# Full expert tiles: one 512-column product for u's high part against both token parts, score halves added on VectorE, high parts made on ScalarE

## The chip, the cores and the metric

One NeuronCore of a Trainium2 chip runs the whole program. The metric is the device time of one execution in microseconds, the median of several runs. The profile beside it is one execution taken by the hardware profiler.

## The reference

256 tokens of 1024 channels pass one block of attention and feed-forward, and then two layers that each end in a PEER stage. The change lies in the PEER stage. There each token has 8 heads that choose 16 of 16384 experts each; an expert is a row of `u_emb` and a row of `v_emb`, 1024 long:

```python
s = jnp.einsum('thpk,hpnk->thpn', q, sub_keys).astype(jnp.float32)
sv, si = lax.top_k(s, K)
...
gate = jax.nn.softmax(fv, axis=-1)
u = u_emb[eidx]
v = v_emb[eidx]
act = jax.nn.gelu(jnp.einsum('thkd,td->thk', u, x_t).astype(jnp.float32), approximate=False)
return jnp.einsum('thk,thkd->td', (gate * act).astype(x_t.dtype), v)
```

All arrays are float32.

## The kernel before, in words

The kernel gathers nothing. It holds a dense table of gates, 256 tokens by 16384 experts, that is zero where an expert wasn't chosen, and computes every expert for every token. The experts are cut into 128 tiles (TILES) of 128. For a tile j the work is: scores, the product of the tile's u (128 experts x 1024) and the tokens HT (1024 x 256), in 8 steps of 128 channels; Gelu; the product with the tile's gates; values, the product of these activations and the tile's v (128 x 1024), added up in four PSUM banks over all 128 tiles.

For float32 accuracy at the speed of the rounded type (fp32r), an operand is kept as a high part, which is the operand rounded by a copy, and a low part, which is the operand less the high part. A product of two such operands is three matmuls, high by high, high by low and low by high. `in_parts` (L505 is its matmul) issues them. The scores of a full tile are thus 8 x 3 matmuls with 256 columns (the tokens), written to the first half of PSUM bank 4 + j % 2. The values are 4 x 3 matmuls with 512 columns.

A layer's first 26 tiles (EARLY) are treated in another way: their scores are plain float32 products, computed while the experts are being chosen and while the gates are built, and only their values are in parts. The 102 tiles behind them (LATE) are the full tiles: scores and values both in parts. They run in loops of six tiles per turn (STEP) on each engine.

The order of the work in the full tiles is written by hand for each engine:

- TensorE: scores of j+1, values of j, scores of j+2, values of j+1, and so on. Scores wait for the semaphore `expert_u`, values for `expert_gated` and `expert_v`.
- ScalarE (L1216): the Gelu of tile j from PSUM once `expert_scored` tells of it. Nothing else.
- VectorE (`expert`): for tile j, the product with the gates (L1892); the high part of u of tile j+2 once its load has arrived (a cast, `high`, L1799); the high part of the activations; the low part of u of j+2 (`low`, L1803); the low part of the activations, which counts `expert_gated`; then, once values of j-1 are done, the high part and the low part of v of tile j+1.
- SyncE (`load_experts`) issues the loads, 512 KB each: u of n (L2171) once scores of n-3 are done, then v of n (L2178) once values of n-3 are done, then u of n+1, and so on in this one queue.

u and v have three buffers each (E_SLOTS); the low part is written over the loaded operand. The high parts have two buffers each. Plain and rounded names (`ring` and `ring_rounded`, `HN` and `HN_rounded`, `HT` and `HT_rounded`) are the same memory under two types. In `ring`, columns 0 to 3D are u, 3D to 6D v, 6D to 8D the high parts of u, 8D to 10D those of v, 10D to 12D the high part of HT (D is 1024). HN holds the activations and, behind them, `g2_row`. HN and HT are neighbours in memory.

In the early tiles ScalarE makes the high parts of v (L1206), VectorE the low parts.

## Time and profile before

| what | value |
|---|---|
| median of 3 runs | 2453.8 us |
| runs | 2455.82, 2448.6, 2453.8 us |
| profiled execution, span | 2448.3 us |
| TensorE matmul busy | 2366.7 us, 97% |
| VectorE busy | 1939.3 us, 79% |
| ScalarE busy | 547.8 us, 22% |
| mean granted TensorE clock | 0.992 |
| full tiles of layer 1 | from 813 to 1389 us of the span |
| full tiles of layer 2 | from 1858 to 2434 us of the span |

The span runs from the first to the last instruction of the profiled execution; of that execution the profile gives the span alone, and the runs' times lie 0.3 to 7.5 us above it. Busy times are sums over the span. Rows of a timeline give the start in us from the span's start, the duration in us, the engine, the source line, the operation, what it writes and reads, and in brackets how long the engine was idle ahead of it and which work released it. Matmuls are pipelined, so a row with several of them gives the time from the first's start to the last's end, and the spacing of the starts is what one costs in a stream.

### The profile page before, as it was taken

The numbers are of one execution on the slowest core, as the hardware profiler recorded it, in microseconds if no ns is written. First come the engines' busy times: TensorE is split into PE (matmuls) and PEld (weight loads), VectorE is DVE, ScalarE is ACT, GpSimd is POOL, SyncE is SP. The second block draws the span as 40 slices with busy tenths as digits, with TensorE's granted clock in tenths as the row PEclk, the third lists the DMA queues.
The fourth block names the chain that finished last, engine by engine and source line by source line (L and its number), as shares of the span: only waits on it lengthen the run. The fifth ranks groups of instructions, "written<-read, shape, count | busy, mean of one in ns | idle before, by whom it ended". The sixth has DMA issues, their size and how long they took to land.

```text
span 2448.3 us, 38882 instructions
## 1 busy us (share of the span) xinstructions
PE 2366.7 (97%) x14368; PEld 2061.1 (84%) x14368; DVE 1939.3 (79%) x3972; ACT 547.8 (22%) x962; POOL 298.2 (12%) x228
## 2 busy tenths in 40 slices
PE   8998999999999999999999998999999999999998
PEld 7766998669887899999999877698978999999997
DVE  5445887769997888888888766399987888888887
ACT  4433332222333100000000236223331000000001
POOL 0000000026580000000000000266800000000000
PEclk9999999999999999999999999999999999999999
DMA  7324888853215455555555550232154555555553
GB/s 270 150 78 155 301 325 332 338 226 130 87 36 198 164 187 183 186 184 187 188 188 188 207 186 35 103 121 88 43 180 164 188 187 184 184 185 187 187 188 129
DMA packets 97731, 430.08 MB, mean 176 GB/s; under 512 B 11232, under 2 KB 11872, under 8 KB 90720
## 3 DMA queue, kind: packets, MB, share of 16 engines
q1 hardware_dynamic: 97632, 428.75, 48.6%
q8 instruction: 63, 1.03, 0.2%
q14 instruction: 36, 0.29, 0.0%
HBM read 427.66 MB, written 1.05 MB: 175 GB/s over the span
## 4 chain that ended last, share of the span: by engine, by line
PE 83%; DVE 13%; ACT 2%; DMA 1%; issue 1%; SPq 0%; DVEq 0%; ACTq 0%; PEldq 0%
PE ps L505 66%; PE ps L550 5%; PE ps L773 4%; DVE HN L1785 4%; DVE HN L1783 3%; PE ps L563 3%; PE ps L600 1%; PE ps L621 1%; DVE arena L1795 1%; PE ps L735 1%; DVE ring_rounded L1803 1%; PE ps L799 1%; ACT arena L1012 1%; DMA ring<-in_stream 1%; DVE ring_rounded L1374 1%
## 5 line engine op out<-in xcount | busy, mean ns | idle before, releaser
L505 PE MATMUL ps<-ring_rounded,HN_rounded 128*128 128x512 f32 (+1 forms) x3104 | 751.2, 391 | 8.6 <-DVE ring_rounded L1803 5.2
L505 PEld LDWEIGHTS ps<-ring_rounded,HN_rounded 128*128 128x128 f32 x3104 | 567.0, 188 | 127.2 <-issue 15.0
L505 PE MATMUL ps<-ring_rounded 128*128 128x256 f32 x3264 | 619.4, 283 | 0.0
L1803 DVE TENSOR_TENSOR ring_rounded<-ring,ring_rounded 128x1024 fp32r<-128x1024 f32 x460 | 561.9, 1222 | 19.2 <-ACT ring_rounded L1206 12.0
L505 PEld LDWEIGHTS ps<-ring_rounded 128*128 128x128 f32 x3264 | 522.3, 191 | 7.9
L505 PE MATMUL ps<-HT_rounded,ring_rounded 128*128 128x256 f32 x1632 | 461.8, 283 | 0.0
L1799 DVE CAST ring_rounded<-ring 128x1024 fp32r<-128x1024 f32 x406 | 280.5, 691 | 151.3 <-DMA ring<-in_experts_u 149.4
L505 PEld LDWEIGHTS ps<-HT_rounded,ring_rounded 128*128 128x128 f32 x1632 | 312.5, 191 | 7.9
L1216 ACT ACTIVATE HN<-ps 128x256 f32<-128x256 f32 x204 | 78.5, 385 | 1061.7 <-PE ps L505 1061.7
L505 PE MATMUL ps<-parts 128*128 128x256 f32 (+2 forms) x1184 | 249.2, 301 | 1.9 <-DVE parts L1369 1.5
L773 PE MATMUL ps<-HT,ring 128*128 128x256 f32 x832 | 202.5, 381 | 1.4 <-ACT arena L982 1.4
L505 PEld LDWEIGHTS ps<-parts 128*128 128x128 f32 x1184 | 192.1, 189 | 12.8 <-DVE parts L1369 2.0
L2120 POOL TENSOR_TENSOR ring_rounded<-ring,parts 128x1024 fp32r<-128x1024 f32 x8 | 18.8, 2376 | 1375.8 <-ACT parts L1158 1375.8
L2134 POOL TENSOR_SCALAR HN<-iota,slots_t 128x128 f32<-128x128 f32 x128 | 177.5, 1389 | 64.2 <-DVEq L1775 36.2
L773 PEld LDWEIGHTS ps<-HT,ring 128*128 128x128 f32 x832 | 148.9, 192 | 16.6 <-ACT arena L982 1.8
L505 PE MATMUL ps<-parts,ring_rounded 128*128 128x256 f32 x576 | 162.3, 282 | 0.0
L1374 DVE TENSOR_TENSOR ring_rounded<-ring,parts 128x4096 fp32r<-128x4096 f32 (+2 forms) x28 | 117.5, 4198 | 44.5 <-ACT parts L1005 44.0
L799 PEld LDWEIGHTS ps<-HN 128*128 128x128 f32 x1024 | 131.5, 194 | 24.0 <-issue 13.7
L799 PE MATMUL ps<-HN 128*128 128x128 f32 x1024 | 141.1, 282 | 7.2 <-DVE HN L1785 5.8
L1892 DVE TENSOR_TENSOR HN<-HN,arena 128x256 f32<-128x256 f32 x204 | 130.6, 640 | 16.1 <-ACT HN L1216 11.1
L550 PE MATMUL ps<-ring,HT 128*128 128x512 f32 (+1 forms) x320 | 136.2, 586 | 0.0
L982 ACT ACTIVATE arena<-ps 128x512 f32<-128x512 f32 (+4 forms) x136 | 77.3, 580 | 221.5 <-PE ps L505 144.9
(254 smaller groups left out, 2566.8 us busy)
## 6 DMA issues: line engine op xcount, KB each, us to landing
ring<-in_experts_u SPq DMA_DIRECT2D x256, 512.0 KB, 4.2
ring<-in_experts_v SPq DMA_DIRECT2D x256, 512.0 KB, 3.5
ring<-in_stream SPq DMA_DIRECT2D x45, 2048.0 KB, 8.8
arena<-in_ada SPq DMA_DIRECT2D x96, 512.0 KB, 7.2
arena<-in_keys SPq DMA_DIRECT2D x2, 1024.0 KB, 13.9
ring<-in_stream SPq DMA_DIRECT2D x1, 1792.0 KB, 7.9
ring<-in_stream SPq DMA_DIRECT2D x1, 1664.0 KB, 8.1
ring<-in_stream SPq DMA_DIRECT2D x1, 1040.0 KB, 19.1
```

Source lines behind the costliest of these rows:

```text
L505: mm = pe.matmul(out_, p, q, start=(first and i == 0), stop=(last and i == 2))
L550: mm = pe.matmul(t[:, 0:n], src[:, k, b * P:(b + 1) * P], w[:, k, :], start=(k == 0), stop=(k == nk - 1))
L773: mm = pe.matmul(ps[:, 4 + n % 2, 0:T], pre_u[:, n % P_SLOTS, k * P:(k + 1) * P], HT[:, k, :], start=(k == 0), stop=(k == KT - 1))
L799: mm = pe.matmul(ps[:, 6 + u, t * P:(t + 1) * P], hot[:, u, 1, t, :], hot[:, u, 0, t, :], start=True, stop=True)
L982: ins = act.activation(dst, t if src is None else src(t), func)
L1216: act.activation(act_e[:, a, :], ps[:, 4 + a, 0:T], ACT.Gelu).then_inc(sem("expert_act"), 1)
L1374: dve.tensor_tensor(weights_low(name), weights(name)[:, 0:IN_PARTS_SIZE[name]], weights_high(name).bitcast(F32), ALU.subtract).then_inc(se ...
L1785: ins = dve.tensor_scalar(hot[:, u, 1, t, :], iota, slots_t[:, 1, at_ + t:at_ + t + 1], slots_t[:, 2, at_ + t:at_ + t + 1], ALU.is_equal, ...
L1799: return dve.tensor_copy(dst, src)
L1803: return dve.tensor_tensor(dst, src, h.bitcast(F32), ALU.subtract)
L1892: dve.tensor_tensor(act_e[:, j % 2], act_e[:, j % 2], g, ALU.mult).then_inc(sem("split_steps"), 1)
L2134: pool.tensor_scalar(hot[:, g % 2, 1, GROUP - 1, :], iota, slots_t[:, 1, t:t + 1], slots_t[:, 2, t:t + 1], ALU.is_equal, ALU.mult).then_in ...
```

## The change

In the full tiles:

- `HN_rounded` and `HT_rounded` become one tensor, so that one operand (`ht_both`) can name both token parts: the high part moves from `ring` to HN, the low part stays in HT. For each of the 8 channel steps the high part of u meets both token parts in one matmul of 512 columns, which fills a whole PSUM bank: the first half has high by high, the second half high by low. The low part of u meets the high token part in a matmul of 256 columns that is added to the first half. So 24 matmuls of 256 columns become 8 of 512 and 8 of 256.
- The two halves still have to be added. ScalarE copies the second half to SBUF (`half_s`), VectorE adds the first half to it, and the Gelu works on that sum in SBUF.
- The high parts of u (tile j+2) and of v (tile j+1) are made by ScalarE instead of VectorE.
- ScalarE's order for tile j is now: half copy, wait for u of j+2 and its high part, Gelu, wait for v of j+1 and its high part. VectorE's order is: low part of v of j, the add, the low part of u of j+2, the product with the gates, the high part and the low part of the activations.
- The activations and the half copy now lie in `ring` from 10D on, and `g2_row` in `arena`.

SyncE's program isn't changed.

```diff
--- before.py
+++ after.py
@@ -142,7 +142,8 @@
                   ("arena", T * NKEYS))
         with ExitStack() as whole_floats:
             hn_flat, ht_flat, ring, arena = [whole_floats.enter_context(nc.sbuf_tensor(name, [P, n], F32))[:, :] for name, n in shared]
-        hn_r, ht_r, ring_r = [sb(f"{name}_rounded", n, F32R)[:, :] for name, n in shared[:3]]
+        hnht_r, ring_r = sb("HNHT_rounded", NB * D + KT * T, F32R)[:, :], sb("ring_rounded", SLOTS * SLOT, F32R)[:, :]
+        hn_r, ht_r = hnht_r[:, 0:NB * D], hnht_r[:, NB * D:]
         parts_at = 13600
         act_parts_r = sb("act_parts", 2 * FT * T, F32R)[:, :]
         sb("arena_before", parts_at - 2 * FT * T)
@@ -465,14 +466,15 @@
         exp_vh = r3(ring_r[:, 8 * D:10 * D], 2)
         meanwhile = r3(ring[:, 0:3 * D], GATE_TILES)
         pre_u = r3(ring[:, 6 * D:10 * D], P_SLOTS)
-        ht_high = r3(ring_r[:, 10 * D:12 * D], KT)
-        ht_low = r3(ht_r, KT)
-        act_e = r3(hn_flat[:, 0:512], 2)
-        act_l = r3(hn_r[:, 0:512], 2)
-        act_h = r3(hn_r[:, 512:1024], 2)
-        g2_row = hn_flat[:, 1024:2048]
+        ht_high, ht_low = r3(hn_r, KT), r3(ht_r, KT)
+        ht_both = hnht_r.rearrange("p (a k t) -> p a k t", a=2, k=KT)
+        act_e = r3(ring[:, 10 * D:10 * D + 512], 2)
+        act_l = r3(ring_r[:, 10 * D:10 * D + 512], 2)
+        act_h = r3(ring_r[:, 10 * D + 512:11 * D], 2)
+        half_s = r3(ring[:, 11 * D:11 * D + 512], 2)
         g2_diag = arena[:, 0:D]
         end_diag = arena[:, D:2 * D]
+        g2_row = arena[:, 2 * D:3 * D]
         hot = hn_flat.rearrange("p (u a t n) -> p u a t n", u=2, a=2, t=GROUP)
         NG = T // GROUP
 
@@ -811,10 +813,11 @@
                 def expert_scores(j, ready):
 
                     pe.wait_ge(sem("expert_u"), ready)
+                    t = ps[:, 4 + j % 2, :]
                     for k in range(KT):
                         c = slice(k * P, (k + 1) * P)
-                        mm = in_parts(ps[:, 4 + j % 2, 0:T], (exp_uh[:, j % 2, c], exp_ul[:, j % E_SLOTS, c]),
-                                           (ht_high[:, k, :], ht_low[:, k, :]), k == 0, k == KT - 1)
+                        pe.matmul(r3(t, 2), exp_uh[:, j % 2, c], ht_both[:, :, k, :], start=(k == 0), stop=False)
+                        mm = pe.matmul(t[:, 0:T], exp_ul[:, j % E_SLOTS, c], ht_high[:, k, :], start=False, stop=(k == KT - 1))
                     mm.then_inc(sem("expert_scored"), 1)
 
                 def expert_values(j, ready, first=False, last=False, low=None):
@@ -1198,22 +1201,48 @@
                             keep_scores(n)
                     if g == NG - 6:
                         act.wait_ge(sem("expert_v0_arrived"), 16 * (l * len(range(0, TILES, E_SLOTS)) + 1))
-                        act.activation(exp_vh[:, 0], exp_v[:, 0], ACT.Copy).then_inc(sem("early_v_high"), 1)
+                        act.activation(exp_vh[:, 0], exp_v[:, 0], ACT.Copy).then_inc(sem("v_high"), 1)
                 for n in range(1, EARLY + 1):
                     act.wait_ge(sem(f"expert_v{n % E_SLOTS}_arrived"), 16 * (l * len(range(n % E_SLOTS, TILES, E_SLOTS)) + n // E_SLOTS + 1))
                     if n >= 2:
                         act.wait_ge(sem("expert_used"), l * (TILES + 1) + n)
-                    act.activation(exp_vh[:, n % 2], exp_v[:, n % E_SLOTS], ACT.Copy).then_inc(sem("early_v_high"), 1)
+                    act.activation(exp_vh[:, n % 2], exp_v[:, n % E_SLOTS], ACT.Copy).then_inc(sem("v_high"), 1)
                     if SPLIT_AT <= n < SPLIT_AT + KT:
                         k = n - SPLIT_AT
                         act.activation(ht_high[:, k], HT[:, k], ACT.Copy).then_inc(sem("ht_high"), 1)
                     if n == G2_AT + 2:
                         act.wait_ge(sem("g2_spread"), l + 1)
                         act.activation(g2_row, ps[:, 6:8, :].rearrange("p a n -> p (a n)"), ACT.Copy).then_inc(sem("g2_row"), 1)
-                with act.Fori(0, LATE // 2) as i:
-                    for a in range(2):
-                        act.wait_ge(sem("expert_scored"), i * 2 + (l * TILES + EARLY + a + 1))
-                        act.activation(act_e[:, a, :], ps[:, 4 + a, 0:T], ACT.Gelu).then_inc(sem("expert_act"), 1)
+
+                def expert(j, turn=None):
+
+                    def at_(n, each=1):
+                        return n if turn is None else turn * (STEP * each) + n
+
+                    def arrived(kind, n):
+
+                        count = 16 * (l * len(range(n % E_SLOTS, TILES, E_SLOTS)) + n // E_SLOTS + 1) if kind == "v" else \
+                            16 * (l * LATE // E_SLOTS + (n - EARLY) // E_SLOTS + 1)
+                        act.wait_ge(sem(f"expert_{kind}{n % E_SLOTS}_arrived"), count if turn is None else turn * (16 * STEP // E_SLOTS) + count)
+
+                    act.wait_ge(sem("expert_scored"), at_(l * TILES + j + 1))
+                    act.activation(half_s[:, j % 2], ps[:, 4 + j % 2, T:2 * T], ACT.Copy).then_inc(sem("half_stored"), 1)
+                    if j + 2 < TILES:
+                        arrived("u", j + 2)
+                        act.activation(exp_uh[:, j % 2], exp_u[:, (j + 2) % E_SLOTS], ACT.Copy).then_inc(sem("u_high"), 1)
+                    act.wait_ge(sem("expert_summed"), at_(l * LATE + j - EARLY + 1))
+                    act.activation(act_e[:, j % 2], act_e[:, j % 2], ACT.Gelu).then_inc(sem("expert_act"), 1)
+                    if j + 1 < TILES:
+                        arrived("v", j + 1)
+                        act.wait_ge(sem("expert_used"), at_(l * (TILES + 1) + j + 1))
+                        act.activation(exp_vh[:, (j + 1) % 2], exp_v[:, (j + 1) % E_SLOTS], ACT.Copy).then_inc(sem("v_high"), 1)
+
+                turns = (LATE - 2) // STEP
+                with act.Fori(0, turns) as i:
+                    for j in range(STEP):
+                        expert(EARLY + j, i)
+                for j in range(EARLY + turns * STEP, TILES):
+                    expert(j)
                 load_table(ACT.Sqrt)
 
 
@@ -1818,7 +1847,7 @@
                 def early_v_low(n):
 
                     v_arrived(n)
-                    dve.wait_ge(sem("early_v_high"), l * (EARLY + 1) + n + 1)
+                    dve.wait_ge(sem("v_high"), l * TILES + n + 1)
                     low(exp_vl[:, n % E_SLOTS] if low_in_place(n) else exp_uh[:, n % 2], exp_v[:, n % E_SLOTS], exp_vh[:, n % 2]).then_inc(sem("expert_v"), 1)
 
                 def split_ht_part(k):
@@ -1877,48 +1906,38 @@
                         diagonal(f"g2_{l}", g2_diag, mod(l, 5))
                         if l == 1:
                             diagonal("end2", end_diag, col("final_norm_2"), factor=-0.5)
-                dve.wait_ge(sem("expert_used"), base_v + EARLY)
-                early_v_low(EARLY)
-
-                def expert(j, turn=None, more_u=True, more_v=True):
+
+                def expert(j, turn=None):
 
                     def at_(n, each=1):
                         return n if turn is None else turn * (STEP * each) + n
 
                     n = at_(j - CHOICE_TILES)
-                    done = split_base + 4 * (j - EARLY)
+                    done = 2 * (l * LATE + j - EARLY)
+                    e = act_e[:, j % 2]
+                    v, vl, vh = exp_v[:, j % E_SLOTS], exp_vl[:, j % E_SLOTS], exp_vh[:, j % 2]
+                    dve.wait_ge(sem("v_high"), at_(base + j + 1))
+                    low(vl, v, vh).then_inc(sem("expert_v"), 1)
+                    dve.wait_ge(sem("half_stored"), at_(l * LATE + j - EARLY + 1))
+                    dve.tensor_tensor(e, ps[:, 4 + j % 2, 0:T], half_s[:, j % 2], ALU.add).then_inc(sem("expert_summed"), 1)
+                    if j + 2 < TILES:
+                        u, ul, uh = exp_u[:, (j + 2) % E_SLOTS], exp_ul[:, (j + 2) % E_SLOTS], exp_uh[:, j % 2]
+                        dve.wait_ge(sem("u_high"), at_(l * (LATE - 2) + j - EARLY + 1))
+                        low(ul, u, uh).then_inc(sem("expert_u"), 1)
                     dve.wait_ge(sem("expert_act"), at_(l * LATE + j - EARLY + 1))
                     g = gates[:, :, bass.ds(n, 1)].rearrange("p t o -> p (t o)") if turn is not None else gates[:, :, n]
-                    dve.tensor_tensor(act_e[:, j % 2], act_e[:, j % 2], g, ALU.mult).then_inc(sem("split_steps"), 1)
-                    if more_u:
-                        u, ul, uh = exp_u[:, (j + 2) % E_SLOTS], exp_ul[:, (j + 2) % E_SLOTS], exp_uh[:, j % 2]
-                        u_arrived(j + 2, turn)
-                        high(uh, u).then_inc(sem("split_steps"), 1)
-                    dve.wait_ge(sem("split_steps"), at_(done + 1, 4))
-                    high(act_h[:, j % 2], act_e[:, j % 2]).then_inc(sem("split_steps"), 1)
-                    if more_u:
-                        dve.wait_ge(sem("split_steps"), at_(done + 2, 4))
-                        low(ul, u, uh).then_inc(sem("expert_u"), 1)
-                    dve.wait_ge(sem("split_steps"), at_(done + 2 + more_u, 4))
-                    low(act_l[:, j % 2], act_e[:, j % 2], act_h[:, j % 2]).then_inc(sem("expert_gated"), 1)
-                    if more_v:
-                        v, vl, vh = exp_v[:, (j + 1) % E_SLOTS], exp_vl[:, (j + 1) % E_SLOTS], exp_vh[:, (j + 1) % 2]
-                        v_arrived(j + 1, turn)
-                        dve.wait_ge(sem("expert_used"), at_(base_v + j + 1))
-                        high(vh, v).then_inc(sem("split_steps"), 1)
-                        dve.wait_ge(sem("split_steps"), at_(done + 3 + more_u, 4))
-                        low(vl, v, vh).then_inc(sem("expert_v"), 1)
-
-                split_base = l * (4 * LATE - 3)
+                    dve.tensor_tensor(e, e, g, ALU.mult).then_inc(sem("split_steps"), 1)
+                    dve.wait_ge(sem("split_steps"), at_(done + 1, 2))
+                    high(act_h[:, j % 2], e).then_inc(sem("split_steps"), 1)
+                    dve.wait_ge(sem("split_steps"), at_(done + 2, 2))
+                    low(act_l[:, j % 2], e, act_h[:, j % 2]).then_inc(sem("expert_gated"), 1)
+
                 turns = (LATE - 2) // STEP
                 with dve.Fori(0, turns) as i:
                     for j in range(STEP):
                         expert(EARLY + j, i)
-                for j in range(EARLY + turns * STEP, TILES - 2):
+                for j in range(EARLY + turns * STEP, TILES):
                     expert(j)
-                expert(TILES - 2, more_u=False)
-                split_base -= 1
-                expert(TILES - 1, more_u=False, more_v=False)
                 dve.wait_ge(sem("expert_used"), (l + 1) * (TILES + 1))
                 dve.wait_ge(sem("g2_row"), l + 1)
                 for b in range(NB):
```

## Rows read from the trace of the kernel before

**Rows 1.** The page, the chain that ended last, by line

```profile
PE ps L505 66%; PE ps L550 5%; PE ps L773 4%; DVE HN L1785 4%; DVE HN L1783 3%; PE ps L563 3%; PE ps L600 1%; PE ps L621 1%; DVE arena L1795 1%; PE ps L735 1%; DVE ring_rounded L1803 1%; PE ps L799 1%; ACT arena L1012 1%; DMA ring<-in_stream 1%; DVE ring_rounded L1374 1%
```

**Rows 2.** The chain in order of time: start, duration, what

```profile
813.13 575.97 PE ps L505 x3684
```

**Rows 3.** Stretches: length, busy us PE, PEld, DVE, ACT, POOL, clock, DMA share, GB/s

```profile
740.00:813.00 73.00, 70.78 (x308) 54.91 (x307) 60.33 (x98) 28.96 (x33) 0.00 (x0) 1.00 0.59 196
813.00:1389.00 576.00, 576.00 (x3687) 525.47 (x3686) 485.39 (x709) 41.77 (x105) 0.00 (x0) 1.00 0.51 182
...
1884.00:2434.00 550.00, 550.00 (x3514) 501.51 (x3514) 466.89 (x682) 38.81 (x99) 0.00 (x0) 1.00 0.52 183
```

**Rows 4.** Timeline of TensorE, one period of the full tiles

```profile
1001.30 2.91 PE L505 MATMUL ps<-ring_rounded,HN_rounded 128*128 128x512 f32 x12
1004.04 0.28 PE L505 MATMUL ps<-ring_rounded 128*128 128x256 f32 x1
...
1006.92 2.91 PE L505 MATMUL ps<-ring_rounded,HN_rounded 128*128 128x512 f32 x12
1009.66 0.28 PE L505 MATMUL ps<-ring_rounded 128*128 128x256 f32 x1
```

**Rows 5.** Groups by form, 815 to 1387: busy us, mean ns, idle before

```profile
L1803 DVE TENSOR_TENSOR ring_rounded<-ring,ring_rounded 128x1024 fp32r<-128x1024 f32 x201 | 245.7, 1222 | 3.5
...
L1216 ACT ACTIVATE HN<-ps 128x256 f32<-128x256 f32 x102 | 39.3, 385 | 530.6 <-PE ps L505 530.6
```

**Rows 6.** Timeline of the SP queue, full tiles

```profile
1005.11 0.33 SPq L2171 DMA_DIRECT2D ring<-in_experts_u  x1
1009.86 0.33 SPq L2178 DMA_DIRECT2D ring<-in_experts_v  x1
1010.39 0.33 SPq L2171 DMA_DIRECT2D ring<-in_experts_u  x1
```

**Rows 7.** Timeline of ScalarE and VectorE, full tiles

```profile
1007.12 0.38 ACT L1216 ACTIVATE HN<-ps 128x256 f32<-128x256 f32 x1 [5.24 <-PE ps L505]
...
1013.26 0.64 DVE L1892 TENSOR_TENSOR HN<-HN,arena 128x256 f32<-128x256 f32 x1
1014.55 0.69 DVE L1799 CAST ring_rounded<-ring 128x1024 fp32r<-128x1024 f32 x1 [0.65 <-DMA ring<-in_experts_u]
...
1016.50 0.42 DVE L1803 TENSOR_TENSOR HN_rounded<-HN,HN_rounded 128x256 fp32r<-128x256 f32 x1
```

**Rows 8.** Timeline of a tile of layer 2 with a late u

```profile
1881.34 0.69 DVE L1799 CAST ring_rounded<-ring 128x1024 fp32r<-128x1024 f32 x1 [2.24 <-DMA ring<-in_experts_u]
...
1883.28 0.42 DVE L1803 TENSOR_TENSOR HN_rounded<-HN,HN_rounded 128x256 fp32r<-128x256 f32 x1
...
1883.76 3.01 PE L505 MATMUL ps<-ring_rounded,HN_rounded 128*128 128x512 f32 x12 [0.24 <-DVE HN_rounded L1803]
...
1886.61 0.28 PE L505 MATMUL ps<-ring_rounded 128*128 128x256 f32 x1
```

**Rows 9.** Groups by form, whole span

```profile
L1206 ACT ACTIVATE ring_rounded<-ring 128x1024 fp32r<-128x1024 f32 x52 | 55.2, 1061 | 93.0 <-PE ps L505 88.3 <-DMA ring<-in_experts_v 4.7
...
L1928 DVE TENSOR_TENSOR arena<-ps,HN 128x512 f32<-128x512 f32 x8 | 5.5, 692 | 7.7 <-PE ps L505 7.2 <-DVE X L1931 0.3
```

**Rows 10.** Timeline of ScalarE and VectorE in the early tiles

```profile
743.38 0.64 DVE L1839 TENSOR_TENSOR HN<-ring,arena 128x256 f32<-128x256 f32 x1
744.05 0.29 DVE L1799 CAST HN_rounded<-HN 128x256 fp32r<-128x256 f32 x1
744.38 0.43 DVE L1803 TENSOR_TENSOR HN_rounded<-HN,HN_rounded 128x256 fp32r<-128x256 f32 x1
...
789.98 1.06 ACT L1206 ACTIVATE ring_rounded<-ring 128x1024 fp32r<-128x1024 f32 x1 [1.55 <-PE ps L505]
...
791.14 1.22 DVE L1803 TENSOR_TENSOR ring_rounded<-ring,ring_rounded 128x1024 fp32r<-128x1024 f32 x1 [0.47 <-ACT ring_rounded L1206]
```

**Rows 11.** Loads issued, 815 to 1387: count, size, median us to landing

```profile
ring<-in_experts_u SPq DMA_DIRECT2D x99, 512.0 KB, 4.3
```

## Prediction

> **What bounds the kernel now.** I read the page first: in the chain that ended last 66% of the span is the matmul line L505 [rows 1]. The chain in order of time says where: one unbroken piece of 575.97 us with 3684 matmuls, the full expert tiles of the first layer [rows 2]. The table of stretches shows the same stage in both layers, TensorE busy 576.00 of 576.00 and 550.00 of 550.00 us at a granted clock of 1.00, VectorE 485 and 467 us, ScalarE 42 and 39 [rows 3]. So TensorE sets this stage, and the change sits in it. The reader should then ask how far away the next limit is.
>
> One tile on TensorE: 24 score products of 256 columns from 1004.04 to 1006.92, 2.88 us or 0.120 each, then twelve value products of 512 columns to 1009.66, 2.74 us or 0.228 each. The period is 5.62 us, from 1001.30 to 1006.92 [rows 4]. A layer has 102 such tiles [rows 5].
>
> Now the loop that is not TensorE's alone. When the values of tile j-2 end (1009.66), SP issues v of j+1 (1009.86) and right behind it u of j+2 (1010.39) [rows 4, 6]. The cast of u waits, with DMA named as releaser, and starts at 1014.55, 4.89 after 1009.66. The low part of the activations of tile j ends at 1016.50 + 0.42 = 1016.92, 2.37 after the landing [rows 7]. Values of j could start about then, while TensorE comes to them only at 1009.66 + 2.88 (scores of j) + 2.74 (values of j-1) + 2.88 (scores of j+1) = 1018.16. So this loop has 1.2 us of slack over two tiles. Once it is seen closing: a u was late, its cast started at 1881.34 after 2.24 idle, the low part ended at 1883.28 + 0.42 = 1883.70, and TensorE, idle 0.24, started the values at 1883.76 and left them at 1886.61 [rows 8].
>
> **The change, part by part.** TensorE's scores become 8 products of 512 columns and 8 of 256. The columns are 6144 as before. By the spacings in [rows 4] they cost 8 x 0.228 + 8 x 0.120 = 2.78 us instead of 2.88: 0.10 saved. Bounds: nothing, if only columns count, and 0.10. TensorE alone could then hold 2.74 + 2.78 = 5.52 us per tile. The Trainium skill (TensorE: Matmul & The Clock Gate, section Back-to-back issue gap) charges N/2.4 + 2.5 ns per warm product; by it the scores would go from 2.62 to 2.60 us, an estimate of 0.02 saved. The rows show a larger part per product that doesn't depend on columns, and they decide.
>
> VectorE loses two casts of 1024 elements (0.69 each, [rows 7]) and gains the add from PSUM. No row has that add at 256 elements; the same kind at 512 takes 0.69 [rows 9], and nothing can be its floor; a low part of 256 without PSUM takes 0.42 [rows 7], so I take 0.45. Its six instructions sum to 1.22 + 0.45 + 1.22 + 0.64 + 0.29 + 0.42 = 4.24 us [rows 5, 7, 10], under 5.5. ScalarE gains two copies of 1024 elements at 1.06 and the half copy, for which the Gelu of the same 256 PSUM columns at 0.385 stands, and makes 2.9 us in all [rows 5, 9]. Neither engine is full.
>
> What matters is what stands behind the wait for u. In ScalarE's new order the copy of u(j+2) waits for its landing, and behind it stand the Gelu of tile j and the high part of v(j+1). In VectorE's new order the low part of u(j+2) waits for ScalarE's copy, and behind it stand the gate product, the high and the low part of the activations of tile j. Before, the Gelu and the gate product were done ahead of the landing (gate product at 1013.26, landing at 1014.55), and behind it came only a cast of 0.69 that overlaps the next one, the low part of u and the low part of the activations [rows 7]. Now all of it comes behind. The Trainium skill (TensorE: Matmul & The Clock Gate, the table at the top) calls the queues of ScalarE and VectorE strict FIFO; the written order in the rows agrees.
>
> From the landing to the gated activations, after the change:
> - landing to start, 0.02, and ScalarE's copy of u, 1.06 [rows 9];
> - handing over to VectorE, between 0.03 (743.38 + 0.64 to 744.05, within VectorE) and 0.10 (789.98 + 1.06 to 791.14) [rows 10]; I take 0.06;
> - low part of u, 1.22 [rows 5];
> - gate product, high, low, each waiting for the one ahead: 743.38 to 744.38 + 0.43, 1.43 [rows 10], less 0.02 of overlap with the instruction ahead.
>
> Sum 3.77, against 2.37 before. The Gelu (0.385, right after ScalarE's copy) hides under the low part of u, 1.22. The half copy and the add hide ahead of the landing: 0.2 to the start as for the Gelu now (1006.92 to 1007.12, [rows 4, 7]), 0.385, 0.1 and at most 0.69 make 1.4 us after the scores, and u lands 2.0 or more after them (1014.55 against 1012.54). Uncovered they would cost 1.2. ScalarE's high part of v(j+1) ends 1.08 + 0.385 + 1.06 = 2.5 after the landing and is read after 3.77: hidden; it waits for the values of j-1, over by then. SP's queue is untouched: u is still issued behind v. The first score product of the next tile but one needs the low part of u(j+2), ready 2.4 after the landing and wanted some 6 later.
>
> From the end of the low part of the activations to the end of the values: 1883.70 to 1886.61, 2.91 us [rows 8].
>
> The landing: u is issued 0.73 after the values end (1009.66 to 1010.39) and lands 4.3 later in the median; once in six tiles SP's loop turns and it is 1.07 (1004.04 to 1005.11) [rows 4, 6, 11]. Mean (5 x 0.73 + 1.07)/6 + 4.3 = 5.09.
>
> Loop over two tiles: 5.09 + 3.77 + 2.91 = 11.77 us, 5.885 per tile; TensorE needs only 2 x 5.52 = 11.04. The landing of u then sets the stage, and since a late landing isn't wholly made good by an early one I take 5.89. Loss: 5.89 - 5.62 = 0.27 us, from the second full tile to the third from last, 99 per layer, 198: 53.5 us. At a layer's end the last activations have no tile to hide behind; half copy and add lengthen that by some 0.5 each time, 1 us. The moves of the activations, of g2_row and of the HT parts are the same instructions in other columns: nothing, and under TensorE's products in the stage before anyway (70.78 busy of 73, [rows 3]); if g2_row came late it would cost its one 1 us copy.
>
> The profiled execution has a span of 2448.3 us; with 54.5 that is 2502.8. The runs read 2448.6 to 2455.82, 0.3 to 7.5 above this span, and their median 2453.8 is 5.5 above. Predicted: 2453.8 + 54.5 = 2508 us.
>
> **The rivals.**
> 1. TensorE stays the bound and the saving is real. The loop would have to fit in 11.04 us, 0.73 less than the sum. For it: VectorE and ScalarE are far from full by the totals. Against it: every term but the handover is a row. Time: 0.10 x 204 = 20 less, 2434 us.
> 2. No change: the columns are all that TensorE pays for, and u lands early enough, or the loop comes to about the old 11.24, 0.5 less than the sum (landing within 4.6 rather than 5.1). For it: one landing in the rows, 1010.39 to 1014.55, took 4.16 and not 4.3. Time 2447 to 2460. The Trainium skill's formula above would give it too, 0.02 x 204 = 4 us, if TensorE stayed the bound.
> 3. Slower still: ScalarE and VectorE compute their wait counts from the loop register. With 0.1 more on each of three handovers and u landing in 4.5, the loop is 12.3 us, 6.13 per tile: 0.51 x 198 = 101, 2555 us; half of it, 2530.
>
> **How the numbers follow.** My forecast has a chance of 0.74. Its own range, from the bounds: handovers -0.05 to +0.15 and landing 4.1 to 4.5 make -0.25 to +0.35 per two tiles, 5.76 to 6.07 per tile, 2482 to 2543 us. Rival 1 has 0.10, rivals 2 and 3 have 0.08 each. To hold 8 in 10 the range is 2460 to 2545: the forecast, the upper edge of rival 2 and the near half of rival 3. A measurement of this kernel tells 0.3%, 7.4 us, from no change. Faster: rival 1, 0.10. Same: rival 2, 0.08. Slower: forecast and rival 3, 0.82.
>
> **What would show it.** Right: in the stage TensorE idles ahead of the value products with VectorE's low part of the activations as releaser, some 0.3 us per tile; ScalarE's copy of u has DMA as releaser and the Gelu starts as that copy ends; the period is near 5.9 and the chain runs through DMA, ScalarE and VectorE. Wrong: TensorE busy all the stage, period 5.5 or 5.6. The step most at risk is the landing: at 4.4 us after the values, not 5.1, the loss is gone. A fall of the granted clock under the new gaps would break the sum upward; from 740 to 813, where TensorE already waits 3% of the time, it stays at 1.00 [rows 3].

## The result and the profile after

| | median us | runs us | ratio to before |
|---|---|---|---|
| before, on the same chip | 2452.44 | 2448.6 to 2455.82 | |
| changed | 2501.9 | 2501.89 to 2508.08 | 1.0207, 95% interval 1.0193 to 1.0222 |

The change makes the kernel 49.5 us slower (four runs of each kernel). The forecast was 54.5 us slower, 2508 us, with a range of 2460 to 2545.

The page of the changed kernel, its chain by line, against [rows 1]:

```profile
PE ps L507 34%; DMA ring<-in_experts_u 14%; PE ps L552 5%; PE ps L775 4%; DVE HN L1814 4%; PE ps L819 3%; ACT ring_rounded L1232 3%; DVE ring_rounded L1832 3%; DVE HN L1812 3%; PE ps L565 2%; DVE ring L1929 2%; PE ps L820 2%; PE ps L602 1%; DVE ring_rounded L1828 1%; SPq L2197 1%
```

The loads of u, which are not among the lines of [rows 1], now make 14% of the chain. Stretches, columns as in [rows 3]:

```profile
740.00:813.00 73.00, 70.63 (x308) 54.83 (x307) 60.39 (x98) 28.98 (x33) 0.00 (x0) 1.00 0.59 196
815.00:1390.00 575.00, 563.48 (x2751) 460.52 (x2749) 389.68 (x588) 266.14 (x392) 0.00 (x0) 1.00 0.50 178
1890.00:2470.00 580.00, 565.47 (x2766) 463.30 (x2765) 393.69 (x593) 268.44 (x394) 0.00 (x0) 1.00 0.50 179
```

The early tiles (740 to 813) are unchanged. In the full tiles TensorE now idles 11.5 of 575 us at the same clock of 1.00, and no other engine is near full: VectorE has less to do than in [rows 3] (390 against 485 us) and ScalarE six times as much (266 against 42). A reader of totals alone would see little that explains a slower kernel: 11.5 us are 0.12 us per tile, and the period has grown by 0.24. Busy time hides the rest, because the row of a product of 256 columns lasts 0.28 us while the next product can start 0.12 us after it [rows 4]. The spacing of the starts shows the whole stall, as TensorE's rows below do. The waits between 820 and 1400 do (engine, line, what it waited for: total us, times, longest):

```profile
DVE ring_rounded L1832 <- ACT ring_rounded L1232: 178.0, 99, 3.2
ACT ring_rounded L1232 <- DMA ring<-in_experts_u: 172.0, 99, 2.6
ACT ring L1229 <- PE ps L820: 138.1, 99, 1.7
PEld ps L507 <- DVE ring_rounded L1832: 33.1, 72, 1.5
PE ps L507 <- DVE ring_rounded L1832: 10.5, 27, 1.1
```

Read from the bottom: TensorE's value products wait for VectorE's low part, VectorE waits for ScalarE's copy of u in every one of 99 tiles, and that copy waits for the load in every one. 99 tiles in 580 us is 5.86 us per tile, against 5.62 in [rows 4].

The chain in order of time shows one lap of the loop, two tiles long:

```profile
996.58 4.34 DMA ring<-in_experts_u
...
1000.93 1.07 ACT ring_rounded L1232
...
1002.03 0.37 DVE ring_rounded L1832
...
1003.17 0.64 DVE ring L1929
...
1003.83 0.31 DVE ring_rounded L1828
...
1004.16 0.43 DVE ring_rounded L1832
...
1004.64 3.04 PE ps L507 x12
...
1007.70 0.33 SPq L2197
...
1008.23 4.29 DMA ring<-in_experts_u
...
1012.54 1.07 ACT ring_rounded L1232
```

Load of u, ScalarE's copy, low part of u, gate product, high part, low part of the activations, values, SP with v ahead of u, the next load of u. From one load to the next it is 1008.23 - 996.58 = 11.65 us. The timeline of ScalarE in the same stretch, and of TensorE:

```profile
1004.57 0.38 ACT L1229 ACTIVATE ring<-ps 128x256 f32<-128x256 f32 x1 [1.32 <-PE ps L820]
1006.43 1.06 ACT L1232 ACTIVATE ring_rounded<-ring 128x1024 fp32r<-128x1024 f32 x1 [1.47 <-DMA ring<-in_experts_u]
1007.39 0.40 ACT L1234 ACTIVATE ring<-ring 128x256 f32<-128x256 f32 x1
```

```profile
1004.26 0.28 PE L820 MATMUL ps<-HNHT_rounded,ring_rounded 128*128 128x256 f32 x1
1004.64 3.03 PE L507 MATMUL ps<-ring_rounded 128*128 128x512 f32 x12
1007.51 0.39 PE L819 MATMUL ps<-HNHT_rounded,ring_rounded 128*128 128x512 f32 x1
```

Half copy, 1.47 us of waiting for the load, the copy of u, and only then the Gelu (L1234). The values start 0.38 us after the last score product (1004.26 to 1004.64) where 0.12 would do, so TensorE loses 0.26 us ahead of them; the forecast had said some 0.3 per tile, with VectorE's low part as releaser. They run to 1007.51, 2.87 us; before they took 2.74 [rows 4].

### The profile page after: what moved, and what is told of

Its sections match the earlier page's. It is cut to its first block, busy times and chain, and to the rows that moved or that the text cites. A ratio compares the mean times of both kernels' runs of the same rounds, so it can differ in the third digit from the quotient of the medians.

```text
span 2500.1 us, 35824 instructions
## 1 busy us (share of the span) xinstructions
PE 2392.6 (96%) x12736; PEld 1973.6 (79%) x12736; DVE 1777.2 (71%) x3774; ACT 1018.3 (41%) x1568; POOL 298.8 (12%) x228
## 3 DMA queue, kind: packets, MB, share of 16 engines
q8 instruction: 62, 1.02, 0.2%
## 4 chain that ended last, share of the span: by engine, by line
PE 56%; DVE 18%; DMA 15%; ACT 5%; issue 4%; SPq 1%; DVEq 0%; ACTq 0%; PEldq 0%
PE ps L507 34%; DMA ring<-in_experts_u 14%; PE ps L552 5%; PE ps L775 4%; DVE HN L1814 4%; PE ps L819 3%; ACT ring_rounded L1232 3%; DVE ring_rounded L1832 3%; DVE HN L1812 3%; PE ps L565 2%; DVE ring L1929 2%; PE ps L820 2%; PE ps L602 1%; DVE ring_rounded L1828 1%; SPq L2197 1%
## 5 line engine op out<-in xcount | busy, mean ns | idle before, releaser
L1832 DVE TENSOR_TENSOR ring_rounded<-ring,ring_rounded 128x1024 fp32r<-128x1024 f32 (+1 forms) x688 | 643.3, 959 | 382.7 <-ACT ring_rounded L1232 356.8
L507 PE MATMUL ps<-ring_rounded 128*128 128x512 f32 x3072 | 760.9, 398 | 35.5 <-DVE ring_rounded L1832 32.0
L507 PEld LDWEIGHTS ps<-ring_rounded 128*128 128x128 f32 x3072 | 558.8, 188 | 201.5 <-DVE ring_rounded L1832 71.7
L819 PE MATMUL ps<-HNHT_rounded,ring_rounded 128*128 128x512 f32 x1632 | 582.6, 397 | 0.0
L820 PE MATMUL ps<-HNHT_rounded,ring_rounded 128*128 128x256 f32 x1632 | 457.4, 280 | 0.0
L819 PEld LDWEIGHTS ps<-HNHT_rounded,ring_rounded 128*128 128x128 f32 x1632 | 306.6, 188 | 73.3
L1232 ACT ACTIVATE ring_rounded<-ring 128x1024 fp32r<-128x1024 f32 x200 | 212.1, 1061 | 341.4 <-DMA ring<-in_experts_u 341.4
L820 PEld LDWEIGHTS ps<-HNHT_rounded,ring_rounded 128*128 128x128 f32 x1632 | 307.8, 189 | 7.9
L1238 ACT ACTIVATE ring_rounded<-ring 128x1024 fp32r<-128x1024 f32 x202 | 212.0, 1049 | 10.7 <-PE ps L507 10.2
L1229 ACT ACTIVATE ring<-ps 128x256 f32<-128x256 f32 x204 | 78.5, 385 | 287.1 <-PE ps L820 287.1
L801 PEld LDWEIGHTS ps<-HN 128*128 128x128 f32 x1024 | 131.5, 194 | 23.9 <-issue 10.5
L1008 ACT ACTIVATE parts<-ring 128x4096 fp32r<-128x4096 f32 (+2 forms) x28 | 96.5, 3446 | 103.8 <-PE ps L507 85.9
```

Source lines behind the costliest of these rows:

```text
L507: mm = pe.matmul(out_, p, q, start=(first and i == 0), stop=(last and i == 2))
L801: mm = pe.matmul(ps[:, 6 + u, t * P:(t + 1) * P], hot[:, u, 1, t, :], hot[:, u, 0, t, :], start=True, stop=True)
L819: pe.matmul(r3(t, 2), exp_uh[:, j % 2, c], ht_both[:, :, k, :], start=(k == 0), stop=False)
L820: mm = pe.matmul(t[:, 0:T], exp_ul[:, j % E_SLOTS, c], ht_high[:, k, :], start=False, stop=(k == KT - 1))
L1232: act.activation(exp_uh[:, j % 2], exp_u[:, (j + 2) % E_SLOTS], ACT.Copy).then_inc(sem("u_high"), 1)
L1238: act.activation(exp_vh[:, (j + 1) % 2], exp_v[:, (j + 1) % E_SLOTS], ACT.Copy).then_inc(sem("v_high"), 1)
```

## The experiments

Each run has its own runs of the kernel before on the same chip. Edits are against the changed kernel.

**1. Both orders turned round.** On ScalarE the Gelu goes ahead of the copy of u, on VectorE the activations go ahead of the low part of u.

```diff
 # ScalarE
+act.wait_ge(sem("expert_summed"), ...)
+act.activation(act_e[:, j % 2], act_e[:, j % 2], ACT.Gelu).then_inc(sem("expert_act"), 1)
 if j + 2 < TILES:
     arrived("u", j + 2)
     act.activation(exp_uh[:, j % 2], exp_u[:, (j + 2) % E_SLOTS], ACT.Copy).then_inc(sem("u_high"), 1)
-act.wait_ge(sem("expert_summed"), ...)
-act.activation(act_e[:, j % 2], act_e[:, j % 2], ACT.Gelu).then_inc(sem("expert_act"), 1)
 # VectorE, behind the add
-if j + 2 < TILES:
-    dve.wait_ge(sem("u_high"), ...)
-    low(ul, u, uh).then_inc(sem("expert_u"), 1)
 dve.wait_ge(sem("expert_act"), ...)
...
 low(act_l[:, j % 2], e, act_h[:, j % 2]).then_inc(sem("expert_gated"), 1)
+if j + 2 < TILES:
+    dve.wait_ge(sem("u_high"), ...)
+    low(ul, u, uh).then_inc(sem("expert_u"), 1)
```

> The changed kernel with two orders turned round: on ScalarE the Gelu of tile j stands ahead of the high part of u of j+2, and on VectorE the gate product and the two parts of the activations stand ahead of the low part of u. Nothing else differs. Theory (the wait for u's landing stands ahead of the activations): the loop through the landing is gone, TensorE is the bound again with the 2.81 us of scores and 2.75 of values seen without a stall in the changed kernel, 5.56 per tile against 5.62 before, so 0.06 x 204 = 12 us under before, 2440 us, and 60 us under the changed kernel. Rival (the work added to VectorE and ScalarE, their PSUM reads or the split product itself cost the time, and the order doesn't matter): within 10 us of the changed kernel, 2490 to 2510. If only part of the loss is the order, it lands between, 2455 to 2490.

Measured: 2446.33 us, ratio to before 0.9973, interval 0.9962 to 0.9985. With both orders turned round the whole loss is gone, and 6 us more. The time is 6 us above the 2440 expected, and the timeline of TensorE shows where:

```profile
999.82 2.94 PE L507 MATMUL ps<-ring_rounded 128*128 128x512 f32 x12
1002.60 0.39 PE L819 MATMUL ps<-HNHT_rounded,ring_rounded 128*128 128x512 f32 x1
...
1005.41 1.80 PE L507 MATMUL ps<-ring_rounded 128*128 128x512 f32 x7
```

Scores 2.81 us, values 2.78, period 5.59 without a stall. The values take 0.04 more than in [rows 4] (2.74); 0.03 us for 204 tiles is the 6 us. Experiments 7 and 8 ask why.

ScalarE still waits for the load of u in this kernel, between 820 and 1380:

```profile
ACT ring_rounded L1234 <- DMA ring<-in_experts_u: 78.9, 99, 1.5
```

That wait costs nothing now: no wait of TensorE stands in the same table any more, since the activations are ahead of the wait and not behind it.

**2. ScalarE's order alone** (the first half of that diff).

> The changed kernel with ScalarE's order alone turned round: the Gelu ahead of the high part of u. VectorE still makes the low part of u, which waits for the landing and ScalarE's copy, ahead of the gate product. Theory: the Gelu was hidden under the low part of u anyway, so nothing moves: 2498 to 2506 us. Rival (it is ScalarE's queue that delays the activations): near 2440.

Measured: 2499.47 us, ratio 1.0197, interval 1.018 to 1.0214, as the theory had it. The Gelu behind the copy was covered by VectorE's low part of u.

**3. VectorE's order alone** (the second half).

> The changed kernel with VectorE's order alone turned round: gate product and activations' parts ahead of the low part of u. The Gelu still stands behind ScalarE's copy of u, which waits for the landing. Theory: from landing to gated activations it is now 0.02 + 1.06 + 0.385 + 0.14 + 1.43 = 3.03 us instead of 3.77, the loop over two tiles 5.09 + 3.03 + 2.91 = 11.03, just under the 11.12 that TensorE needs, so TensorE is nearly the bound and only late landings stall it: 5.58 to 5.66 per tile, 2445 to 2462 us. Rival (order doesn't matter): 2490 to 2510.

Measured: 2456.66 us, ratio 1.0021, interval 1.0011 to 1.0031, inside the 2445 to 2462. ScalarE still waits 172 us for the loads (820 to 1380), as in the changed kernel (820 to 1400), and little of it reaches TensorE:

```profile
ACT ring_rounded L1232 <- DMA ring<-in_experts_u: 171.7, 99, 2.9
...
PEld ps L507 <- DVE ring_rounded L1832: 6.3, 14, 1.0
PE ps L507 <- DVE ring_rounded L1832: 1.5, 5, 0.6
```

In the changed kernel TensorE's weight loads waited 72 times and its products 27 times; here it is 14 and 5. So VectorE's order carries the loss. ScalarE's carries nothing while VectorE's stands (experiment 2), and the last 10 us once VectorE's is mended (2456.66 against 2446.33).

**4. The order of the loads alone.** Both engines keep the changed order; SP issues u of n+1 ahead of v of n. The cut shows the loop; the six tiles ahead of it have the same edit, and the last six are written out behind it.

```diff
-fetch_u(s, u[...n...], i * STEP + (base + n - E_SLOTS + 1))
+fetch_u((s + 1) % E_SLOTS, u[...n + 1...], i * STEP + (base + n - E_SLOTS + 2))
 fetch_v(s, v[...n...], i * STEP + (base_v + n - E_SLOTS + 2))
```

> The changed kernel with only the order of the loads turned round: SP issues u of n+1 ahead of v of n, so that u no longer stands behind a load that waits for values of n-3 and goes out as soon as scores of n-2 are done. Both engines keep the changed order. Theory: u is issued some 3.2 us earlier, has landed by the time that scores of tile j end, and the loop through it falls under 9 us per two tiles; TensorE is the bound, 5.56 to 5.60 per tile, 2440 to 2450 us. Rival (the longer chain on VectorE and ScalarE behind the scores is the cause, whatever the landing): 2480 or more.

Measured: 2446.41 us, ratio 0.9981, interval 0.9967 to 0.9994. Breaking the loop at its other end gives the same time as experiment 1. ScalarE's timeline:

```profile
1006.49 0.39 ACT L1229 ACTIVATE ring<-ps 128x256 f32<-128x256 f32 x1 [1.69 <-PE ps L820]
1006.77 1.05 ACT L1232 ACTIVATE ring_rounded<-ring 128x1024 fp32r<-128x1024 f32 x1
1007.72 0.40 ACT L1234 ACTIVATE ring<-ring 128x256 f32<-128x256 f32 x1
```

The copy of u starts as the half copy ends, with no wait. The chain of instructions on the engines is as long as in the changed kernel, so its length alone is not the cause.

**5. The high parts on ScalarE alone**, with 24 score products as before, in the changed orders.

```diff
-pe.matmul(r3(t, 2), exp_uh[:, j % 2, c], ht_both[:, :, k, :], start=(k == 0), stop=False)
-mm = pe.matmul(t[:, 0:T], exp_ul[:, j % E_SLOTS, c], ht_high[:, k, :], start=False, stop=(k == KT - 1))
+mm = in_parts(t[:, 0:T], (exp_uh[:, j % 2, c], exp_ul[:, j % E_SLOTS, c]), (ht_high[:, k, :], ht_low[:, k, :]), k == 0, k == KT - 1)
 # ScalarE: no half copy, the Gelu reads PSUM; VectorE: no add
```

> One half of the change alone: the high parts of u and v are made by ScalarE, in the changed orders, but the scores stay 24 products of 256 columns, so there are no half copy and no add (the Gelu reads PSUM, still behind ScalarE's copy of u). Theory: from landing to gated activations it is the same 3.77 us, the loop over two tiles the same as in the changed kernel (11.73 measured there), against 2 x 5.62 that TensorE needs; period 5.86, as the changed kernel or up to 5 us above it: 2498 to 2508 us. Rival (the split product, the half copy and the add carry the loss): near before, 2450 to 2465.

Measured: 2500.7 us, ratio 1.0203, interval 1.0181 to 1.0224: all of the loss without the split product.

**6. The split product, half copy and add alone**, with the high parts on VectorE in the order of the kernel before and the add ahead of the gate product.

```diff
 # VectorE, expert(j) of the kernel before
+dve.wait_ge(sem("half_stored"), ...)
+dve.tensor_tensor(act_e[:, j % 2], ps[:, 4 + j % 2, 0:T], half_s[:, j % 2], ALU.add).then_inc(sem("expert_summed"), 1)
 dve.wait_ge(sem("expert_act"), ...)
 # ScalarE: half copy and Gelu only
```

> The other half alone: the split product, the half copy and the add, with the high parts of u and v on VectorE in its old order, the add put ahead of the gate product. Theory, from rows: on VectorE the wait-free time from the gate product of one tile to the end of the low part of v is 5.51 less 0.65 of waiting, 4.86 us; the add, the Gelu that VectorE has to wait for and the handovers put 0.98 ahead of it: 5.84 us per tile, over the 5.59 that TensorE needs, so VectorE is the bound and the time is 2453 + 0.22 x 204 = 2498 us, 2485 to 2505. The loop through the landing has slack here (5.09 + 2.37 + 2.91 = 10.4). Rival (VectorE overlaps more than the rows show; TensorE stays the bound): 2446 to 2452.

Measured: 2472.16 us, ratio 1.0082, interval 1.0063 to 1.0101. The direction was right and the size was not; 2472 lies outside 2485 to 2505. VectorE's timeline:

```profile
1004.51 0.42 DVE L1914 TENSOR_TENSOR ring<-ps,ring 128x256 f32<-128x256 f32 x1
1005.52 0.65 DVE L1917 TENSOR_TENSOR ring<-ring,arena 128x256 f32<-128x256 f32 x1 [0.59 <-ACT ring L1231]
...
1010.23 0.42 DVE L1914 TENSOR_TENSOR ring<-ps,ring 128x256 f32<-128x256 f32 x1
```

VectorE has no wait but the 0.59 for the Gelu in each tile, and its period is 1010.23 - 1004.51 = 5.72 us, over TensorE's 5.59: it is the bound in this order. TensorE's weight loads wait for its low parts 88 times between 820 and 1380:

```profile
PEld ps L507 <- DVE ring_rounded L1825: 17.4, 88, 0.2
```

Without the 0.59 of waiting VectorE would need 5.72 - 0.59 = 5.13 us, an estimate, less than TensorE's 5.59. An order that puts other work of VectorE's between the add and the gate product was not tried.

From add to gate product it is 1.01, as expected (0.98); from gate product to the next add 4.71, where 4.86 had been worked out by taking a wait off a stretch of the kernel before.

**7. High parts on ScalarE, both orders turned round, 24 score products**: experiment 5 with the orders of experiment 1.

> As the run with the high parts alone, but with both orders turned round (the Gelu ahead of ScalarE's copy of u; the gate product and the activations' parts ahead of VectorE's low part of u). Scores are 24 products of 256 columns, activations lie where the change puts them. TensorE should be the bound. It tells why the value products take 2.783 us in the two TensorE-bound runs against 2.748 before. If the place of the activations does it: values 2.783, scores 2.872, period 5.655, 2459 us. If the score products ahead of them do it (the first value products behind a run of products are slower, and the run differs): values 2.748, period 5.62, 2452 us, as before. In both cases far from 2500.

Measured: 2451.06 us, ratio 0.9988, interval 0.9977 to 0.9999. TensorE's timeline has the values at [rows 4] again:

```profile
1000.24 2.91 PE L507 MATMUL ps<-ring_rounded 128*128 128x512 f32 x12
1002.99 3.04 PE L507 MATMUL ps<-HNHT_rounded,ring_rounded 128*128 128x256 f32 x24
1005.86 1.32 PE L507 MATMUL ps<-ring_rounded 128*128 128x512 f32 x5
```

Values 2.75, scores 2.87, period 5.62. The place of the activations costs nothing; the score products ahead of the values do. Against experiment 1 the split product as written is worth about 0.03 us per tile by the periods, 5 us by the medians; the intervals of the two ratios overlap a little (from 0.9977 to 0.9985).

**8. The score products grouped**: experiment 1, and TensorE issues the eight products of 512 columns and then the eight of 256.

```diff
 for k in range(KT):
     c = slice(k * P, (k + 1) * P)
     pe.matmul(r3(t, 2), exp_uh[:, j % 2, c], ht_both[:, :, k, :], start=(k == 0), stop=False)
+for k in range(KT):
+    c = slice(k * P, (k + 1) * P)
     mm = pe.matmul(t[:, 0:T], exp_ul[:, j % E_SLOTS, c], ht_high[:, k, :], start=False, stop=(k == KT - 1))
```

> As the first run (both orders turned round), but TensorE issues the eight products of 512 columns first and then the eight of 256, instead of in turns. What is at issue is why the split product gave 0.06 us on the scores and took 0.035 back on the values. If it is the alternation of the two widths (a product of 512 costs 0.235 behind one of 256, against 0.227 in a run of its own kind): scores 8 x 0.228 + 8 x 0.120 = 2.78, values 2.748 behind a run of 256s as before, period 5.53, 2446 - 0.065 x 204 = 2433 us. If the split product costs what it does whatever the order: 5.593 and 2446 us.

Measured: 2429.37 us, ratio 0.9915, interval 0.9901 to 0.9928.

```profile
1000.81 1.98 PE L819 MATMUL ps<-HNHT_rounded,ring_rounded 128*128 128x512 f32 x8
1002.63 1.12 PE L822 MATMUL ps<-HNHT_rounded,ring_rounded 128*128 128x256 f32 x8
1003.58 2.91 PE L507 MATMUL ps<-ring_rounded 128*128 128x512 f32 x12
1006.33 0.84 PE L819 MATMUL ps<-HNHT_rounded,ring_rounded 128*128 128x512 f32 x3
```

Scores 2.77 us, values 2.75, period 5.52. The 2433 us expected were 4 us too many. This version beats both kernels: 24 us under before and 72 under the change as it was made.

**9. The grouped products in the changed kernel**, with the changed orders.

> The changed kernel, orders of ScalarE and VectorE as changed, with only the score products grouped (eight of 512 columns, then eight of 256), which took 0.08 us per tile, 17 us in all, off the kernel with turned orders. Theory (the landing of u sets the period, not TensorE): all of that gain is lost in TensorE's waits, 2496 to 2504 us, the waits ahead of the value products longer by what the scores are shorter. Rival (the loss is a cost on top of TensorE's own work): 17 us less than the changed kernel, near 2484.

Measured: 2503.37 us, ratio 1.02, interval 1.0176 to 1.0225. The median is the changed kernel's within the noise, so the time saved on TensorE has gone into its waits. Between 820 and 1400 the wait of its products ahead of the values doubled, from 10.5 us; that of its weight loads, 33.1 before, stayed:

```profile
PEld ps L507 <- DVE ring_rounded L1834: 33.9, 57, 1.4
PE ps L507 <- DVE ring_rounded L1834: 21.7, 48, 1.2
```

The traced execution is the longest of the four (2511.53 us), so the size of these waits is less sure than their place.

**10. No half copy and no add** (what it leaves out is in its expectation).

> The changed kernel without the half copy and the add: the split product is computed, but its second half (high part of u by low part of the tokens) is left out of the scores, the Gelu reads the first half from PSUM, in the same place of ScalarE's order. Theory: half copy and add end some 0.9 us ahead of the landing of u, so leaving them out gives nothing but the ends of the two layers: 2498 to 2504 us. Rival (they lie on the path, 0.8 us or more per two tiles): 2430 to 2470.

Measured: 2501.42 us, ratio 1.0199, interval 1.0175 to 1.0222. These are two runs only, but the rival's 2430 to 2470 is far off. The two instructions were covered.

**11. Both mendings of experiments 1 and 4 together.**

> Both engines' orders turned round as in the first run, and u issued ahead of v as in the fourth. Each alone made TensorE the bound without a stall, at 5.593 us per tile. Theory: together nothing more, 5.593 per tile, 2444 to 2449 us, 0.2 to 0.3% under before. Rival (each of them still hid some stall of the other kind, or u and v no longer overlapping slows a load): more than 0.1% away from either.

Measured: 2447.03 us, ratio 0.9982, interval 0.997 to 0.9993. Either one is enough.

## Why the prediction was right

**What bounds.** TensorE before, the loop through the landing of u after. Shown from two sides: the loop opened on the engines (experiment 1) and opened at the loads (experiment 4) both give back the whole loss, and a saving on TensorE gives nothing while the loop is closed (experiment 9).

**The terms of the loop**, two tiles:

| term | predicted us | measured us | from |
|---|---|---|---|
| end of values to start of the copy of u | 5.11 | 5.12 in the mean of 96 tiles, 5.03 in the lap shown | 820 to 1390; 1007.51 to 1012.54 |
| copy of u to end of the low part of the activations | 3.75 | 3.66 | 1000.93 to 1004.16 + 0.43 |
| of it, handing over to VectorE | 0.06 | 0.03 to 0.04 | 1000.93 + 1.06 to 1002.03 |
| from there to the end of the values | 2.91 | 2.94 in the mean, 2.92 in the lap shown | 820 to 1390; 1004.59 to 1007.51 |
| period | 5.89 | 5.86 | 99 tiles in 580 us |

The three means add up to 11.72, twice the period. Loss by the measured period: (5.86 - 5.62) x 198 = 47.5 us, and the 1 predicted for the ends, against 49.5 measured. The prediction's excess of 5 us over the measured step is the 0.03 us per tile. It comes from the chain between landing and gated activations, 0.09 too long: handing over is at its lower bound, and the copy and the instructions behind it overlap a little more than was counted. The step called most at risk, the landing, came out as priced. It spreads, though, from 4.85 to 5.99 us after the values, with a median of 5.02; the mean sets the period and one lap does not.

The 1.2 us of slack that the prediction gave the kernel before is an upper value. By the prediction's own terms that loop takes 5.09 + 2.37 + 2.91 = 10.37 of 11.24 us, a slack of 0.9. The forecast doesn't use it.

**TensorE's saving.** Mis-sized: 0.10 us per tile was predicted, 5.52 in all. As written the product saves 0.06 on the scores and gives back 0.04 on the values, period 5.59. It didn't enter the sum since TensorE wasn't the bound; it would have put rival 1 at 2446 and not at 2434. Grouped, the same products reach 5.52 (experiment 8), so the row of a uniform run was the right price for a uniform run and the wrong one for an alternating one. The Trainium skill (TensorE: Matmul & The Clock Gate, section Back-to-back issue gap) has a formula that knows only a product's own width, by which the prediction estimated 0.02 us saved. The section calls it the gap of an isolated product and says that it comes out too high at 512 columns in a stream of weight loads and products; the prediction left that out. Here the stream's spacing at 512 is 0.228 us (1000.81 to 1002.63 for eight, experiment 8), above the formula's 0.216. Experiments 1 and 8 differ in the order of the products alone, and by 14 us (ratios 0.9973 and 0.9915) to 17 us (medians), which a formula of that form cannot give; the measurement decides.

**What was costed at nothing.** Half copy and add: covered (experiment 10). The Gelu behind ScalarE's copy: covered while VectorE's order stands (experiment 2). The add, estimated at 0.45, took 0.42. The new places: nothing (experiment 7). ScalarE's high part of v: no wait of VectorE's on it stands among the stage's long ones.

**What the engines' totals say.** Moving the high parts to ScalarE is of use: without the move, and in the one order tried, the split product makes VectorE the bound (experiment 6, 2472 us). That the move is needed in any order is not shown. With the move, the loss is gone once the instructions that wait for u stand behind the activations, or once u is issued earlier.

**The rivals.** Rival 1 (TensorE stays the bound) is what experiments 1 and 4 make true, not the change. Rival 2 is ruled out by the interval. Rival 3's longer handovers are not there; its 2530 us is the point half way between the forecast and its 2555, not half of its loss.

## What to carry to other kernels

When work moves to an idle engine, write down for both engines what stands behind each wait, and add up the loop from one load to the next rather than the busy time per tile: here every engine had room, and an instruction that is wanted six microseconds later held up four that were wanted at once. Put the instruction that waits for a load last in its tile, or issue its load earlier; either one was worth 55 us here. In a stream of matmuls of two widths, try them grouped by width: here it was worth about three times the split product itself.

## What the runs showed of the hardware

- The spacing of matmuls depends on what ran ahead. Eight products of 512 and eight of 256 take 2.81 us in turns and 2.77 in two groups, and the twelve value products behind them 2.78 against 2.75. Columns and count are the same; what in TensorE makes the difference wasn't tried.
- A load of 512 KB of u lands 4.3 us after its issue when v is issued half a microsecond ahead of it, and 3.4 when the loads are issued 2.8 to 3.0 us apart (experiment 4, medians in the table of loads between 820 and 1380):

```profile
ring<-in_experts_v SPq DMA_DIRECT2D x99, 512.0 KB, 3.4
ring<-in_experts_u SPq DMA_DIRECT2D x98, 512.0 KB, 3.4
```
